# Latents' and grouped value projections placed behind the first scores of their attentions, keys ahead of queries

## The chip, the core and the metric

The program runs on one core of one Trainium2 chip. Five engines work side by side, each on its own stream of instructions, and meet only at semaphores: TensorE (PE) does matmuls and transposes, VectorE (DVE), ScalarE (ACT) and GpSimd (POOL) do the elementwise work, and SyncE (SP) issues the loads of the weights. The metric is the device time of one execution in microseconds (us); lower is better. Three runs of the kernel before gave 2188.7, 2191.41 and 2195.02, so the median is 2191.41.

## What is computed

The program runs two blocks one after the other. The first (window attention, memory attention, routed experts, twice) is not touched. The second works on 256 latent tokens and 256 context tokens of 1024 values in two layers. The part that matters here:

```python
h  = modulate(rmsnorm(x,  norm1_g[i]), sh1,  sc1)      # latents
hc = modulate(rmsnorm(xc, norm1_g[i]), csh1, csc1)     # context
# layer 0: differential attention, 8 heads, each with two maps of 64 values
q, k, v = split(t @ w_in, 3)           # for t = h and for t = hc
q, k = axial_rope(rmsnorm(q, q_norm)), axial_rope(rmsnorm(k, k_norm))   # latents only
a = softmax(q0 k0') - lam * softmax(q1 k1')
o = rmsnorm(a @ v, subln) * (1 - lambda_init)          # y = o @ w_out
# latents attend to context and latents (512 keys), the context to itself (256)
# layer 1: grouped attention, 8 query heads of 128 values over 2 key heads; only the latents' output
s = softmax(q k' / sqrt(128)); o = s @ v
```

Behind each attention comes `w_out`, a gated residual, a norm and a gated feed-forward network.

## The kernel before

All products of activations and weights are float32 in three passes: the weights and the activations are split in a high part (`w_hi`, `at_hi`) and a rest (`w_lo`, `at_lo`). A weight tile is 128x2048 floats (1 MB). SP loads it in one of 4 `raw` slots, ACT makes `w_hi` (L1426), POOL makes `w_lo` (L644, four pieces), and PE uses it from a ring of 3 slots. A tile is one quarter of a 1024x1024 projection.

The order of the work is written out by hand, once per engine, and every engine runs its stream in that order. In layer 0 (`context_and_latents`) it is:

1. the context's values (`gemm`), its keys (`heads_t(4, 0, ...)`), the transposes of the latents' normed rows into `at_hi`/`at_lo` (`to_at(HL)`), one small transpose (`columns`, L959), and the context's queries (`heads_t(0, 4, ...)`);
2. the context's attention (`diff_attention(0)`), after which DVE norms its output rows (L2177 to L2185, 128x1024 each, once per row tile) and transposes feed them to a second pair of activations;
3. the latents' values V1 (`gemm(1)`), the transposes of the context's output (`to_at(HC)`), the latents' values V2, the context's output projection D1, `tables(0)`, the second half D2, then the latents' four key tiles K0 to K3 and four query tiles Q0 to Q3 in one call, `heads_t(4, 4, 0, True)`;
4. the transposes of the context rows for its feed-forward, and the latents' attention (`diff_attention(1)`).

`heads_t` runs a tile's matmuls (`gemm_t`), ACT writes squares and a copy of them (L1697, L1699), and one tile later PE sums the squares with `ones` (L784 for a key, L791 for a query) and, with `turned`, multiplies by `swap` (L794) for the rope: `sums(j)`. For a key ACT takes the root (L1687), and DVE then works L2199, L2206 twice, L2210 and L2211; for a query DVE works L2206 twice and L2213, and one column scale at the end (L2224, L2225) serves all queries.

The bank ring: the results of `gemm_t`, of transposes and of scores go to four PSUM banks in turn. `wb_wait` lets PE write the n-th only when DVE (or the softmax) has freed the one four before it; `wb_freed` counts the freed ones in order. So a transpose behind three key tiles needs the first of them to be through DVE, and so on.

`tables(0)` spreads the rope table: DVE copies `TAB` into `PB` twice (L2235), PE transposes four pieces (L810), and DVE copies the result back (L2238). PE stands at `transpose_src()` until DVE has signalled.

`attention` is a pipeline over 16 pairs of head and row tile: in step `it` PE does the scores of `it` (L979; L1385 in layer 1), the transposes of the probabilities of `it-2` (L902) and the product with the values of `it-3` (L988, L1396). DVE takes maxima (L2302, L2326), ACT exponentials (L1564), DVE combines (L2343, L2354). Layer 1 runs `to_at(HL)`, one value tile (`gemm(1, 256)`), `tables(1)`, one key tile and four query tiles (`heads_t(1, 4, 1, True)`) and then its attention.

Of the kernel before, what the change touches and what calls it, by code (L numbers as in the profile page):

```python
# [31 lines left out]
P = 128  # L32
TOK = 256
NT = TOK // P
D = 1024
# [35 lines left out]
def gated_tiles(n_f):  # L71
# [8 lines left out]
         + 6 + 4 + gated_tiles(F_FFN // P))  # L80

# [99 lines left out]
def build(nc, A, out):  # L181
    ctx = ExitStack()
    with ctx:
# [136 lines left out]
        def q_bank(k_tiles):  # L320

            return head_bank(k_tiles, 0)
# [103 lines left out]
        def _(sp):  # L426
# [186 lines left out]
            by256(diff_in, 0, D)  # L613
            gemm(diff_in, 2 * D, 3 * D)
            gemm(diff_out, 0, D)
            by256(diff_in, D, 2 * D)
            by256(diff_in, 0, D)
# [4 lines left out]
            cols256(gqa_in, D + 256)  # L622
            cols256(gqa_in, D)
            by256(gqa_in, 0, D)
            gemm(gqa_out, 0, D)
# [40 lines left out]
        def _(pe):  # L666
# [104 lines left out]
            def heads_t(k_tiles, q_tiles, wide, turned, at=0, odd=0):  # L771


                freed, free = c.get("wb"), c.get("y")

                def sums(j):
# [4 lines left out]
                    if j >= 2:  # L781
                        pe.wait_ge(wb_freed, freed + j - 1)
                    if j < k_tiles:
                        ins = pe.matmul(head_bank(j + odd, 0), ones[wide][:, :], head_squares[j % 2], start=True, stop=True)  # L784
                    else:
                        per = 1 if wide else 2
                        own = ones[wide][:, 0:1] if wide else ones[wide][:, 0:P:64]
                        for b in range(2):
                            for t in range(NT):
                                c0 = t * 16 + (2 * (j - k_tiles) + b) * per  # L790
                                ins = pe.matmul(q_bank(k_tiles)[:, c0:c0 + per], head_squares[j % 2][:, b * TOK + t * P:b * TOK + (t + 1) * P],  # L791
                                                own, start=True, stop=True)
                    if turned:
                        ins = pe.matmul(head_bank(j, 1), swap[wide][:, :], head_rows[j % 2], start=True, stop=True)  # L794
# [9 lines left out]
            def tables(wide):  # L804
# [3 lines left out]
                for j in range(4):  # L808
                    src = TAB[:, j % 2 * 256 + j // 2 * P:j % 2 * 256 + j // 2 * P + P] if wide else PB[:, 0, j * P:(j + 1) * P]
# [77 lines left out]
            def attention(n, s_groups, scores, n_chunks, pv, fill=None, queries_last=False):  # L887
# [85 lines left out]
            def diff_attention(path):  # L973
# [18 lines left out]
                attention(16, 2, scores, lambda i: nk // P, pv, queries_last=True)  # L992

            def context_and_latents():
# [5 lines left out]
                columns(1)  # L1000
                heads_t(0, 4, 0, False, at=1)
                diff_attention(0)

                pe.wait_ge(y_freed, c.get("y"))
# [374 lines left out]
            gemm(1, 256)  # L1379
            tables(1)  # L1380
            heads_t(1, 4, 1, True)
# [19 lines left out]
            attention(16, 1, scores, lambda i: 4, pv, queries_last=True)  # L1401
# [7 lines left out]
        def _(act):  # L1409
# [267 lines left out]
            def heads_t(k_tiles, q_tiles, wide, turned, odd=0):  # L1677
# [29 lines left out]
                if q_tiles:  # L1707
                    act.wait_ge(head_summed, c.get("head"))
                    n = q_tiles * (4, 2)[wide]
                    nc.scalar.activation(q_scale[:, :, 0:n], q_bank(k_tiles)[:, 0:NT * 16].rearrange("p (t h) -> p t h", t=NT)[:, :, 0:n],  # L1710
                                         ACT.Sqrt, scale=1.0 / (64, P)[wide], bias=ms[:, 4:5]).then_inc(head_root, 1)

            def diff_attention(path):
                nk = TOK * (1 + path)
                attention(16, 2, lambda i: nk, "diff", None, chunks=lambda i: nk // P)
# [5 lines left out]
            def context_and_latents():  # L1721
# [9 lines left out]
                plain(1)  # L1731
                c.add("wb")
                heads_t(0, 4, 0, False)
                diff_attention(0)
                c.add("y", 2)
                tiles(2)
                to_at(at=1)
                act.dma_start(XC, A["ctx_2"][0].rearrange("(t p) d -> p t d", p=P)).then_inc(x_landed, 16)
                tiles(2)
                c.add("y", 2)  # L1740
                tiles(2)
                plain(1)
                c.add("wb")
                tiles(2)
                rms(XC)
                prm()
                heads_t(4, 4, 0, True)
# [136 lines left out]
            c.add("y", 1)  # L1884
            prm()
            tiles(1)
            plain(1)
            heads_t(1, 4, 1, True)
# [997 lines left out]
```

## Time and profile before

| what | value |
|---|---|
| median of three runs | 2191.41 us (2188.7 to 2195.02) |
| the profiled execution, first to last instruction | 2187.5 us |
| PE busy / DVE / ACT / POOL, us of the span | 1962.1 / 746.8 / 737.2 / 1008.6 |
| mean granted clock of TensorE | 0.944 of full speed |
| layer 0's attention of the context on PE | 1190 to 1231 |
| from there to the latents' attention | 1232 to 1346 |
| latents' attention | 1346 to 1406 |
| layer 1, from its transposes to the end of its attention | 1840 to 1951 |

The profile gives no time of its own for the profiled execution beside the span; the span is 3.9 us under the median of the runs. The stretches that the change touches lie between 1148 and 1406 and between 1840 and 1951. Times in the text are us from the start of the span. A row of a timeline reads: start, duration, engine, line, operation, result, inputs, shapes and count, and in brackets the idle time before it with the engine and line that ended it. A clock of 1.00 is 2.4 GHz, 0.50 is 1.2 GHz, and a value between them is a stretch that saw both.

### The profile page before, as it was taken

What the parts mean: (1) busy time and instruction counts of PE and PEld (TensorE: products, weight loads), DVE (VectorE), ACT (ScalarE), POOL (GpSimd) and SP (SyncE); (2) the same over time, 40 slices, a digit from 0 to 9 for tenths busy, and PEclk for the clock granted to TensorE, in tenths of its full rate; (3) what the DMA queues carried; (4) which work ended last, traced back from release to release, by engine and by line L of the source; (5) the groups of instructions that cost most, each with busy time, mean ns of one, the idle gap of its engine ahead of it and who ended that gap; (6) DMA issues with size and microseconds to landing.
All of it is one profiled execution on the core that took longest, in us unless ns stands there. A gap on an engine that the chain in (4) does not pass through costs nothing. (4 is left out here: it accounts for less than half of the span.)

```text
span 2187.5 us, 29236 instructions
## 1 busy us (share of the span) xinstructions
PE 1962.1 (90%) x11525; PEld 1488.9 (68%) x11525; DVE 746.8 (34%) x1336; ACT 737.2 (34%) x1026; POOL 1008.6 (46%) x784
## 2 busy tenths in 40 slices
PE   7879888999789997999887898999999997887998
PEld 5556654555367774554476686789988997767997
DVE  3453232111433133111244777821163214533112
ACT  3332320011233231111134545544364444444342
POOL 6326500000345630000174284088888886516886
PEclk9979998999899998999997998999999999998999
DMA  7535668999857649999953153056565665304662
GB/s 260 191 115 199 235 253 340 409 409 409 301 205 251 237 169 382 409 409 409 367 167 116 58 184 96 1 155 190 181 181 174 181 190 169 116 10 135 183 185 95
DMA packets 294981, 477.02 MB, mean 218 GB/s; under 512 B 16762, under 2 KB 196973, under 8 KB 294733
## 3 DMA queue, kind: packets, MB, share of 16 engines
q1 hardware_dynamic: 288812, 459.82, 59.5%
q10 hardware_dynamic: 6048, 15.53, 2.0%
q8 instruction: 84, 1.38, 0.3%
q14 instruction: 37, 0.30, 0.0%
HBM read 474.15 MB, written 1.15 MB: 217 GB/s over the span
## 5 line engine op out<-in xcount | busy, mean ns | idle before, releaser
L644 POOL TENSOR_TENSOR w_lo<-raw,w_hi 128x512 fp32r<-128x512 f32 x780 | 1008.4, 1327 | 1162.4 <-ACT w_hi L1426 1162.4
L710 PE MATMUL PS<-at_hi,w_hi 128*128 128x256 f32 x1680 | 488.4, 291 | 20.8 <-DVE at_lo L1935 16.9
L1426 ACT ACTIVATE w_hi<-raw 128x2048 fp32r<-128x2048 f32 x195 | 371.7, 1908 | 344.2 <-PE PS L712 335.8
L711 PE MATMUL PS<-at_lo,w_hi 128*128 128x256 f32 x1680 | 481.2, 286 | 0.0
L712 PE MATMUL PS<-at_hi,w_lo 128*128 128x256 f32 x1680 | 481.1, 286 | 0.0
L710 PEld LDWEIGHTS PS<-at_hi,w_hi 128*128 128x128 f32 x1680 | 328.7, 196 | 35.4 <-DVE at_lo L1935 16.3
L711 PEld LDWEIGHTS PS<-at_lo,w_hi 128*128 128x128 f32 x1680 | 328.7, 196 | 3.7 <-issue 2.6
L712 PEld LDWEIGHTS PS<-at_hi,w_lo 128*128 128x128 f32 x1680 | 328.3, 195 | 0.0
L710 PE MATMUL PS<-w_hi,at_hi 128*128 128x512 f32 (+1 forms) x480 | 192.6, 401 | 31.3 <-DVE at_lo L1935 13.7
L711 PE MATMUL PS<-w_lo,at_hi 128*128 128x512 f32 (+1 forms) x480 | 187.8, 391 | 0.0
L712 PE MATMUL PS<-w_hi,at_lo 128*128 128x512 f32 (+1 forms) x480 | 187.6, 391 | 0.0
L2259 DVE TENSOR_TENSOR PB<-PB,PS 128x256 f32<-128x256 f32 x66 | 27.8, 421 | 363.6 <-ACT PB L1513 363.4
L710 PEld LDWEIGHTS PS<-w_hi,at_hi 128*128 128x128 f32 x480 | 94.8, 198 | 67.7 <-issue 18.3
L712 PEld LDWEIGHTS PS<-w_hi,at_lo 128*128 128x128 f32 x480 | 94.4, 197 | 18.5
L711 PEld LDWEIGHTS PS<-w_lo,at_hi 128*128 128x128 f32 x480 | 95.1, 198 | 17.4 <-issue 0.2
L710 PE MATMUL PS<-w_hi,he_hi 128*128 128x512 f32 x264 | 103.2, 391 | 0.0
L711 PE MATMUL PS<-w_lo,he_hi 128*128 128x512 f32 x264 | 103.1, 390 | 0.0
L712 PE MATMUL PS<-w_hi,he_lo 128*128 128x512 f32 x264 | 102.7, 389 | 0.0
L1145 PE MATMUL PS<-w_plain_hi,KT 128*64 128x512 f32 x224 | 99.2, 593 | 2.0 <-issue 1.2
L678 PE MATMUL PS<-raw,spread_c 128*8 128x512 f32 x384 | 77.2, 700 | 26.1 <-DMA raw<-ada_w 24.6
L1145 PE MATMUL PS<-w_plain_lo,KT 128*64 128x512 f32 x224 | 99.5, 594 | 0.0
L2622 DVE SCALAR_TENSOR_TENSOR at_hi<-PS,st,at_hi 128x1024 fp32r<-128x1024 f32 x16 | 20.5, 1284 | 217.7 <-ACT at_hi L1602 217.7
(312 smaller groups left out, 2499.9 us busy)
## 6 DMA issues: line engine op xcount, KB each, us to landing
raw<-ffn_w_gu SPq DMA_DIRECT2D x132, 512.0 KB, 5.0
raw<-ada_w SPq DMA_DIRECT2D x64, 768.0 KB, 5.3
raw<-ffn_w_down SPq DMA_DIRECT2D x66, 512.0 KB, 4.1
raw<-l_e_up SPq DMA_DIRECT2D x48, 512.0 KB, 15.1
raw<-diff_w_in SPq DMA_DIRECT2D x48, 512.0 KB, 4.6
raw<-l_xkv SPq DMA_DIRECT2D x32, 512.0 KB, 5.6
w_plain_hi<-l_e_gate SPq DMA_DIRECT2D x32, 512.0 KB, 15.0
w_plain_lo<-l_e_gate SPq DMA_DIRECT2D x32, 512.0 KB, 15.3
```

The costliest lines, as they stand in the source:

```text
L644: ins = nc.gpsimd.tensor_tensor(w_lo[:, n % RING, part], raw[:, order_of(n) % RAW, part], w_hi[:, n % RING, part].bitcast(F32), ALU.subtract)
L678: ins = pe.matmul(mod_bank[32 * n:32 * n + 8, :], spread_c[:, a % MOD_TILES, :], raw[:, s % RAW, n * 512:(n + 1) * 512], start=a % MOD_TIL ...
L710: pe.matmul(dst, s_hi, m_hi, start=first, stop=False)
L711: pe.matmul(dst, s_hi, m_lo, start=False, stop=False)
L712: return pe.matmul(dst, s_lo, m_hi, start=False, stop=last)
L1145: ins = pe.matmul(PS[r, bank, :], xe[p % 2][:, 4 * h + k, r], tiles[e][:, k * 512:(k + 1) * 512], start=h == 0 and k == 0, stop=h == 1 and ...
L1426: nc.scalar.activation(w_hi[:, n % RING, :], raw[:, s % RAW, :], ACT.Copy).then_inc(hi_done, 1)
L2259: freed(dve.tensor_tensor(h, silu_buf[:, f % 2, :], b[:, TOK:2 * TOK], ALU.mult))
L2622: dve.scalar_tensor_tensor(o_parts[1].rearrange("p (m n) -> p m n", m=2), PS[:, 6:8, :], st[:, p % 2, 0:1], o_parts[0].bitcast(F32).rearra ...
```

## The change

It moves work and adds a few waits; no product is added or dropped.

- `tables(0)` goes from between D1 and D2 to ahead of the context's queries.
- After the context's attention come K0, K1 and K2, then the transposes of the context's output, then K3, D1, D2 and Q0 to Q3. Before it was V1, transposes, V2, D1, D2, K0 to K3, Q0 to Q3.
- V1 is issued behind the first scores of the latents' attention (`it == 0`) and V2 behind the second (`it == 1`); DVE copies each out to `V` at the same step.
- Layer 1's value tile goes behind the first scores of its attention.
- The `swap` products of the queries all go to one bank, beside the one with the queries' sums, so that `sums(j)` of a query now waits until DVE has freed the tile before it (`freed + j` where it was `freed + j - 1` from `j >= 2`).
- SP loads the weight tiles in the new order.

```diff
-            by256(diff_in, D, 2 * D)
-            by256(diff_in, 0, D)
-            gemm(diff_in, 2 * D, 3 * D)
-            gemm(diff_out, 0, D)
             by256(diff_in, D, 2 * D)
+            gemm(diff_out, 0, D)
             by256(diff_in, 0, D)
+            gemm(diff_in, 2 * D, 3 * D)
...
-                    if j >= 2:
+                    if j >= 1 and j >= k_tiles:
+                        pe.wait_ge(wb_freed, freed + j)
+                    elif j >= 2:
                         pe.wait_ge(wb_freed, freed + j - 1)
...
+                    if it < len(values):
+                        if it:
+                            pe.wait_ge(wb_freed, queries_done)
+                            pe.wait_ge(head_root, c.get("root"))
+                        values[it]()
                     if queries_last and it == 2:
                         pe.wait_ge(wb_freed, queries_done)
+                    if values and it == 2:
+                        pe.wait_ge(y_freed, c.get("y"))
...
                 columns(1)
+                tables(0)
                 heads_t(0, 4, 0, False, at=1)
                 diff_attention(0)
...
-                gemm(1)
-                to_at(HC, wait=False)
-                gemm(1)
-                at_wait()
-                gemm(1, at=1)
-                tables(0)
-                gemm(1, at=1)
-                heads_t(4, 4, 0, True)
+                heads_t(3, 0, 0, True)
+                to_at(HC, wait=False)
+                heads_t(1, 0, 0, True, odd=1 - Y_OUT)
+                pe.wait_ge(wb_freed, c.get("wb") - 1)
+                gemm(1, at=1)
+                at_wait()
+                pe.wait_ge(head_root, c.get("root"))
+                gemm(1, at=1)
+                heads_t(0, 4, 0, True, q_pair=1 - Y_OUT)
                 to_at(HL, wait=False)
                 diff_attention(1)
...
             to_at(HL)
-            gemm(1, 256)
             tables(1)
-            heads_t(1, 4, 1, True)
+            heads_t(1, 4, 1, True, q_pair=1 - Y_GROUPED)
```

Line numbers of the changed kernel differ: its L737 is L730 here, its L820 is L810, L794 is L784, L804 is L794, L996 is L979, and its L717 to L719 are L710 to L712.

On PE, ahead of the context's queries (the transposes of `H` end `to_at(HL)`; `mod_in` and `QT` belong to `columns`). Before:

```order
L730 MATMUL PS<-ident,H 128x128 [waits wb_freed]
L730 MATMUL PS<-ident,H 128x128 x3
L959 MATMUL PS<-ident,QT 128x96 [waits wb_freed,mod_in]
L710 MATMUL PS<-at_hi,w_hi 128x256 [waits lo_done,wb_freed]
L711 MATMUL PS<-at_lo,w_hi 128x256
```

and in the changed kernel:

```order
L737 MATMUL PS<-ident,H 128x128 [waits wb_freed]
L737 MATMUL PS<-ident,H 128x128 x3
L976 MATMUL PS<-ident,QT 128x96 [waits wb_freed,mod_in]
L820 MATMUL PS<-ident,PB 128x128 [waits wb_freed,src_ready]
L820 MATMUL PS<-ident,PB 128x128 x3
L717 MATMUL PS<-at_hi,w_hi 128x256 [waits lo_done,wb_freed]
L718 MATMUL PS<-at_lo,w_hi 128x256
```

The four transposes of the table, with their wait for DVE's two copies, now stand in front of the first query tile.

On DVE, behind the norm of the context's output (its last two operations are the first two rows). Before, the values, the transposed output and the table come next, and the keys much later:

```order
L2182 TENSOR_TENSOR H<-H,hs 128x1024
L2185 TENSOR_TENSOR H<-H,bc 128x1024
L2158 COPY V<-PS 128x512 x2
L1935 TENSOR_TENSOR at_lo<-PS,at_hi 128x4x128 x4
L2158 COPY V<-PS 128x512 x2
L2235 COPY PB<-TAB 128x256 x2
L2238 COPY TAB<-PS 128x512
L2111 TENSOR_TENSOR PB<-PS,PRM 128x512 x2
```

and in the changed kernel, from the third key on (K0 and K1 stand before it in the same four kinds of rows):

```order
L2225 RECIPROCAL PT<-PT 128x512
L2232 SCALAR_TENSOR_TENSOR PT<-PS,gains,TAB 128x512 x2
L2236 TENSOR_TENSOR PT<-PT 128x512
L2237 TENSOR_TENSOR KT<-PT 128x2x256
L1961 TENSOR_TENSOR at_lo<-PS,at_hi 128x4x128 x4
L2225 RECIPROCAL PT<-PT 128x512
```

Three keys' work now lies between the norm and the four `at_lo` of the context's output, and the fourth key's behind them.

On PE, at the head of the latents' attention. Before (the last transposes of the context's rows, then scores of three steps):

```order
L730 MATMUL PS<-ident,H 128x128 x3
L979 MATMUL PS<-KT,QT 128x512 [waits wb_freed,y_freed]
L979 MATMUL PS<-KT,QT 128x512 [waits wb_freed] x5
L902 MATMUL PS<-ident,PB 128x128 [waits t_freed,p_ready,wb_freed]
L902 MATMUL PS<-ident,PB 128x128 x3
```

and in the changed kernel:

```order
L737 MATMUL PS<-ident,H 128x128 x3
L996 MATMUL PS<-KT,QT 128x512 [waits wb_freed,y_freed]
L996 MATMUL PS<-KT,QT 128x512 [waits wb_freed]
L717 MATMUL PS<-w_hi,at_hi 128x512 [waits lo_done,y_freed]
L718 MATMUL PS<-w_lo,at_hi 128x512
```

After the first step's two maps V1 begins (96 matmuls); V2 stands likewise behind the second step's.

## Rows read from the trace of the kernel before

**Rows 1.** The page: the span.

```profile
span 2187.5 us, 29236 instructions
```

**Rows 2.** Busy time by stretch; columns as in the first line.

```profile
core 0: us, PE busy (x) PEld busy (x) DVE busy (x) ACT busy (x) POOL busy (x), PEclk, DMA share, GB/s
1232.00:1278.30 46.30, 46.10 (x214) 38.41 (x215) 26.75 (x27) 15.69 (x13) 34.80 (x27) 1.00 0.48 155
...
1346.50:1363.60 17.10, 14.83 (x32) 6.29 (x32) 12.20 (x27) 12.03 (x27) 0.00 (x0) 0.50 0.14 39
...
1850.30:1860.00 9.70, 8.40 (x49) 8.21 (x49) 0.92 (x4) 1.18 (x1) 0.00 (x0) 0.72 0.20 75
```

**Rows 3.** Timeline of PE ahead of the context's queries.

```profile
1152.57 1.09 PE L730 MATMUL PS<-ident,H 128*128 128x128 f32 x4 [3.28 <-DVE KT L2215]
...
1162.30 0.58 PE L710 MATMUL PS<-at_hi,w_hi 128*128 128x256 f32 x1 [2.38 <-DVE at_lo L1935]
```

**Rows 4.** Timeline of DVE there: the copy of `columns`.

```profile
1164.39 0.26 DVE L2413 COPY modcol<-PS 128x96 f32<-128x96 f32 x1
```

**Rows 5.** The line of the table's copies: ns min/median/max, first and last start.

```profile
L2235 DVE COPY PB<-TAB x2: 1261/3718/6175, 1257.6 to 1263.8; 128x256 f32<-128x256 f32 x2
```

**Rows 6.** Timeline of POOL, near 1164 and during those copies.

```profile
1172.61 2.55 POOL L644 TENSOR_TENSOR w_lo<-raw,w_hi 128x512 fp32r<-128x512 f32 x2 [17.61 <-ACT w_hi L1426]
...
1254.84 13.92 POOL L644 TENSOR_TENSOR w_lo<-raw,w_hi 128x512 fp32r<-128x512 f32 x11
```

**Rows 7.** Timeline of PE behind the context's attention: V1.

```profile
1232.20 0.47 PE L710 MATMUL PS<-w_hi,at_hi 128*128 128x512 f32 x1 [1.04 <-issue]
...
1243.21 1.91 PE L730 MATMUL PS<-ident,H 128*128 128x128 f32 x16
```

**Rows 8.** Timelines of ACT and DVE there: the norm's ends.

```profile
1240.71 0.21 ACT L1471 ACTIVATE hs<-hs 128x8 f32<-128x8 f32 x1 [5.58 <-DVE hs L2179]
...
1242.52 1.22 DVE L2185 TENSOR_TENSOR H<-H,bc 128x1024 f32<-128x1024 f32 x1
```

**Rows 9.** Timeline of PE in the latents' keys.

```profile
1278.13 0.28 PE L710 MATMUL PS<-at_hi,w_hi 128*128 128x256 f32 x1
...
1290.96 0.68 PE L710 MATMUL PS<-at_hi,w_hi 128*128 128x256 f32 x1
...
1298.42 0.68 PE L710 MATMUL PS<-at_hi,w_hi 128*128 128x256 f32 x1
```

**Rows 10.** Timeline of ACT in the keys: the copies, then a split.

```profile
1289.84 0.60 ACT L1697 ACTIVATE PB<-PS 128x512 f32<-128x512 f32 x1 [1.34 <-PE PS L712]
...
1292.15 1.90 ACT L1426 ACTIVATE w_hi<-raw 128x2048 fp32r<-128x2048 f32 x1
```

**Rows 11.** Timeline of DVE: the norm behind D2, then keys.

```profile
1287.61 0.75 DVE L2143 TENSOR_SCALAR H<-H,mv 128x1024 f32<-128x1024 f32 x1
...
1300.17 3.35 DVE L2199 RECIPROCAL PT<-PT 128x512 f32<-128x512 f32 x1
...
1307.65 3.35 DVE L2199 RECIPROCAL PT<-PT 128x512 f32<-128x512 f32 x1
```

**Rows 12.** Timeline of DVE: the last query and the queries' scale.

```profile
1339.52 1.54 DVE L2206 SCALAR_TENSOR_TENSOR PT<-PS,gains,TAB 128x512 f32<-128x512 f32 x2
...
1342.69 0.87 DVE L2225 TENSOR_SCALAR q_scale<-q_scale 128x32 f32<-128x32 f32 x1
```

**Rows 13.** Timeline of PE: the start of the latents' attention.

```profile
1346.49 6.89 PE L979 MATMUL PS<-KT,QT 64*128 64x512 f32 x8 [3.39 <-DVE at_lo L1935]
...
1363.62 0.97 PE L979 MATMUL PS<-KT,QT 64*128 64x512 f32 x2
```

**Rows 14.** Timeline of PE in layer 1.

```profile
1850.36 0.58 PE L710 MATMUL PS<-w_hi,at_hi 128*128 128x256 f32 x1 [8.62 <-DVE at_lo L1935]
...
1859.95 0.66 PE L810 MATMUL PS<-ident,TAB 128*128 128x128 f32 x4 [1.23 <-DVE hs L2231]
...
1906.15 1.09 PE L902 MATMUL PS<-ident,PB 128*128 128x128 f32 x4 [5.47 <-DVE st L2351]
```

**Rows 15.** Timeline of DVE in layer 1: the key begins.

```profile
1874.67 3.35 DVE L2199 RECIPROCAL PT<-PT 128x512 f32<-128x512 f32 x1 [13.26 <-ACT PT L1687]
```

More of the change, by code:

```diff
@@ L769, in gemm_t, with heads_t @@
                     tile_end(ins)
-            def heads_t(k_tiles, q_tiles, wide, turned, at=0, odd=0):
+            def heads_t(k_tiles, q_tiles, wide, turned, at=0, odd=0, q_pair=0):
                 freed, free = c.get("wb"), c.get("y")
+                c.add("root", k_tiles + (q_tiles > 0))
                 def sums(j):
@@ L885, in gated, with attention @@
                 dn(False, True)
-            def attention(n, s_groups, scores, n_chunks, pv, fill=None, queries_last=False):
+            def attention(n, s_groups, scores, n_chunks, pv, fill=None, queries_last=False, values=()):
                 pe.wait_ge(y_freed, c.get("y"))
@@ L991, in pv @@
                         ins.then_inc(o_full, 1)
-                attention(16, 2, scores, lambda i: nk // P, pv, queries_last=True)
+                values = (lambda: gemm(1), lambda: gemm(1)) if path else ()
+                attention(16, 2, scores, lambda i: nk // P, pv, queries_last=True, values=values)
             def context_and_latents():
@@ L1378, in _ @@
             to_at(HL)
-            gemm(1, 256)
             tables(1)
-            heads_t(1, 4, 1, True)
+            assert c.get("y") % 2 == Y_GROUPED
+            heads_t(1, 4, 1, True, q_pair=1 - Y_GROUPED)
             def scores(i, _, bank):
@@ L1400, in pv @@
                     ins.then_inc(o_full, 1)
-            attention(16, 1, scores, lambda i: 4, pv, queries_last=True)
+            attention(16, 1, scores, lambda i: 4, pv, queries_last=True, values=(lambda: gemm(1, 256),))
             pe.wait_ge(y_freed, c.get("y"))
@@ L1714, in diff_attention, with values @@
                 nk = TOK * (1 + path)
-                attention(16, 2, lambda i: nk, "diff", None, chunks=lambda i: nk // P)
+                def values(it):
+                    if path and it < 2:
+                        c.add("y")
+                        tiles(2)
+                attention(16, 2, lambda i: nk, "diff", None, chunks=lambda i: nk // P, fill=values)
                 c.add("y", 4)
@@ L1883, in _, with values @@
             to_at(shifts(0, 1, 0))
-            c.add("y", 1)
             prm()
-            tiles(1)
             plain(1)
-            heads_t(1, 4, 1, True)
-            attention(16, 1, lambda i: 512, "gqa", None, o_at=lambda i: i % 4 == 3, chunks=lambda i: 4,
+            heads_t(1, 4, 1, True, q_pair=1 - Y_GROUPED)
+            def values(it):
+                if it == 0:
+                    c.add("y")
+                    tiles(1)
+            attention(16, 1, lambda i: 512, "gqa", None, o_at=lambda i: i % 4 == 3, chunks=lambda i: 4, fill=values,
                       evac=lambda i: (at_hi[:, 2 * (i // 4):2 * (i // 4) + 2, :], o_bank().rearrange("p (k q) -> p k q", k=2)))
@@ L2185, in head_norm, with heads_t @@
                     (ready if signal else D1)(dve.tensor_tensor(v[:, t, :, :], v[:, t, :, :], g, ALU.mult))
-            def heads_t(k_dsts, q_dsts, gain, wide, turned):
+            def heads_t(k_dsts, q_dsts, gain, wide, turned, odd=0, q_pair=0):
                 first, freed_before = c.get("head"), c.get("wb")
@@ L2287, in gated, with attention @@
                     dve.wait_ge(tile_used, c.get("tile"))
-            def attention(n, s_groups, nk, kind, scale, o_at, o_evac):
+            def attention(n, s_groups, nk, kind, scale, o_at, o_evac, values=()):
                 t0 = c.get("t")
@@ L2361, in attention @@
                         norm(it - 1)
+                    if it < len(values):
+                        values[it]()
                     if 0 <= it - 3 < n and o_at(it - 3):
@@ L2459, in o_evac @@
                                              head_weights[:, own].unsqueeze(2).to_broadcast([P, 4, P]), ALU.mult))
-                attention(16, 2, lambda i: nk, "diff", None, lambda i: i % 4 == 3, o_evac)
+                values = [lambda n=n: y_to([V[:, 2 + u, n * 512:(n + 1) * 512] for u in range(NT)]) for n in range(2 * path)]
+                attention(16, 2, lambda i: nk, "diff", None, lambda i: i % 4 == 3, o_evac, values)
                 dve.wait_ge(y_freed, c.get("y"))
@@ L2811, in _ @@
             dve.wait_ge(tab_landed, 16 * 8)
-            y_to([V[:, 2 + t, 0:256] for t in range(NT)], 256, 1)
-            settled()
             tables(1)
-            heads_t([KT[:, 0:2, TOK:2 * TOK]], [QT[:, 2 * j:2 * j + 2, :] for j in range(4)], G_GK, 1, True)
+            heads_t([KT[:, 0:2, TOK:2 * TOK]], [QT[:, 2 * j:2 * j + 2, :] for j in range(4)], G_GK, 1, True,
+                    q_pair=1 - Y_GROUPED)
             def o_evac(i):
@@ L2819, in o_evac @@
                 o_split(at_hi[:, 2 * j:2 * j + 2, :], at_lo[:, 2 * j:2 * j + 2, :], 2)
-            attention(16, 1, lambda i: 512, "gqa", None, lambda i: i % 4 == 3, o_evac)
+            attention(16, 1, lambda i: 512, "gqa", None, lambda i: i % 4 == 3, o_evac,
+                      [lambda: y_to([V[:, 2 + t, 0:256] for t in range(NT)], 256, 1)])
             a, b8 = affine_of(0, 1, 1)
```

58 lines of the change are left out of this document (29 added, 29 removed).

## The prediction

> **What bounds the kernel now.** I read the page first: the span is 2187.5 us [rows 1], 3.9 under the median of 2191.41, and the chain that ended last is nearly all TensorE. The sum below is a difference inside the profiled execution, added to that median. PE is busy in nearly all of the span, so the question is where it stands still, and at which clock it runs behind that. Second I read PE's waits by stretch, third the timelines of PE and DVE there. What the reader is to see: between the context's attention and the last query PE works without a pause, 46.10 of 46.30 us at clock 1.00 in its first half [rows 2]. It stands still in front of the latents' attention, whose start then runs at clock 0.50 from 1346.5 to 1363.6 with 14.83 of 17.10 us busy [rows 2, 13]. Layer 1 has the same: 8.62 us of waiting, a slow value tile, and 5.47 us of waiting behind the first scores [rows 14]. The change aims the value projections at these holes. They are 22 us and 5.8 us of matmuls, and they do not get shorter by moving; a gain is only what they cover. In their old places they covered something too: DVE's norm of the context's output, and its copies of the table. So I price three places.
>
> **Place 1, the table, ahead of the context's queries.** Before, the first query tile began at 1162.30, behind a wait for `at_lo` [rows 3]. Now PE must also wait for DVE: its copy for `columns` ends at 1164.39 + 0.26 = 1164.65 [rows 4], then come two copies of the table, then PE's transposes, whose start lies 0.42 ahead of the first product in layer 1 (1859.95 there [rows 14]). The delay is (1164.65 - 1162.30) + copies + 0.4 = 2.75 + copies. The copies are the unknown. Before they took 1.26 and 6.18 us for the same 128x256 elements [rows 5], with POOL at work without a gap from 1254.84 for 13.92 us; around 1164 POOL has been idle for most of the 17.61 us that end at 1172.61, as it waits for ACT, which waits for PE [rows 6]. Lower bound: the 0.26 of the 128x96 copy [rows 4] twice, rounded to 0.5. Upper bound: the 7.4 of before. I take 1.2, nearer to the quiet row, since the same copy cannot need both 1.26 and 6.18 for its own work. So +4.0, between +3.3 and +10.2. The old place cost PE nothing (it ran D1 above it), so nothing comes back.
>
> The Trainium skill bears on this ("SBUF — State Buffer", SBUF: two separate sides): VectorE and GpSimd share a port pair as an exclusive lock, and an fp32 copy within SBUF is of the kind that needs it. By that rule the 6.18 is waiting for POOL's pieces, the trace's spread agrees, and place 1 costs the lower figures; without it the delay would be near 10.
>
> **Place 2, keys ahead of values in the latents' part.** I follow both engines from 1231.2, where the attention's last product ends. PE: K0, K1 and the first sums take 12.8 (1278.13 to 1290.96), each further key 7.5 (1290.96 to 1298.42) [rows 9]: 1244.0, then 1251.5. DVE norms the context's output until 1243.7 and ACT is held by it until 1240.9 [rows 8]; ACT then needs two copies of 1.1, a split of 1.9 [rows 10] and a root of 0.7, 4.9 in all, so K0 begins on DVE at 1245.9. A turned key costs DVE 7.5 (1300.17 to 1307.65) [rows 11], as much as PE. So DVE stays late: K0 done at 1253.4, K1 at 1260.9, K2 at 1268.4. Before, PE's 22 us of values gave DVE the time to catch up.
>
> Who waits for it: the transposes of the context's output. The bank ring lets the second to the fourth group of four go only after K0, K1 and K2; that the ring does this is seen ahead of the context's queries, where such a group waited 3.28 for `KT` [rows 3]. PE, free at about 1255, is held until 1268.4. K3's tile wants the bank of the first group, which DVE empties 0.7 later: 1269.1. Behind so long a hole the clock has fallen: in layer 1 one tile behind 8.62 us of waiting took 8.4 at clock 0.72 [rows 2, 14] instead of 5.8. So K3 ends at 1277.5. Then ACT's copies, for which there is no second tile to cover, 1.3, and the sums, 1.3: D1 begins at 1280.1. D1 and D2 are 11.0 each, as V1 was (1232.20 to 1243.21) [rows 7]: 1302.1. DVE's gate and norm behind D2 took until 1288.36 after 1278.13 [rows 9, 11], 10.2, here 1312.3, under the first query tiles. Q0, Q1 and sums: 1314.9; Q2: 1322.4; Q3 with the sums of Q2 (1.8, estimated as a key's with eight small products): 1330.3. The new wait holds the last sums until DVE is through Q2, 2.9: 1333.2; they end at 1335.0, and the last query with the scale takes DVE 4.1 (1339.52 to 1343.56) [rows 12]: 1339.1, which is 4.5 ahead of before.
>
> Now the attention. The scores began 2.9 behind the scale (1346.49) [rows 12, 13]: 1342.0. Two maps at the low clock, the second waiting for its bank, 3.1; V1, 11.0 and 2.6 for the clock as above: 1358.7. Scores 1.2, V2 11.0: 1370.9. Then scores, DVE's copy of V2, one maximum, transposes and the first product with V: I take 6.3, between the 4.2 that this work is at full clock (half of the 8.4 it was busy at clock 0.50) and the 17.1 of the ramp before [rows 2]. The scores of the fifth step begin at 1377.2, before at 1363.62 [rows 13]: +13.6. POOL now works during the first steps and slows DVE's operations a little, +0.4: +14.0. In words: 22 us of values went into the ramp and filled only some 9 of it, and the hole that they left cost more. If the K0 to K2 chain is 3 us shorter or longer, so is this.
>
> **Place 3, layer 1.** The value tile's 9.6 us (1850.36 to 1859.95) [rows 14] leave the front, but its slow start passes to the key: -9.5 + 2.6 = -6.9. The key's sums then run 6.9 earlier, DVE's work on it too: 1874.67 - 6.9 + 7.8 = 1875.6 [rows 15]; the first query's sums, which had no such wait, are due at about 1872.6: +2.9. The last query waits like the latents': +2.9 on PE. Its scale ends at about 1901, 2.5 ahead. Then the value tile, 5.8, stands in the hole of 5.47 [rows 14]; DVE copies it before the second maximum, and the first transposes go at about 1905.7, before at 1906.15. With the better clock behind it: -1.0, between -4 and +3.
>
> **The sum.** 4.0 + 14.0 - 1.0 = +17.0, so 2191.41 + 17.0 = 2208.4; I say 2208. The weights hide: POOL had 17.61 us to spare at place 1, and a hole at PE only lets it get ahead.
>
> **Rivals.**
> A, not slower: the hole between K2 and K3 does not open. It decides at the fourth group of transposes: if DVE is through K2 by 1256 and not at 1268.4, K3 starts at once, its tile runs at full clock and D1 begins 16.6 earlier. Then place 2 is -2.6, the sum +0.4: 2192. For it: 30 us of DVE's work in these keys holds long reciprocals that some other work might let start earlier. Against it: the stream is in order, DVE's norm cannot move, and 7.5 per key stands in four rows running.
> B, slower still: the table's copies take 7.4 as before. It decides on whether the 6.18 was POOL or the operation: sum +23, 2214. Against it are the two durations of one operation.
> C, the low clock stays longer, as it did for the 17.1 us of the ramp, behind the hole in the keys or under V1. By the Trainium skill ("TensorE: Matmul & The Clock Gate", What's actually happening) activity releases the clock again, and a dense tile should recover; rows 2 agree for one tile (0.72). If not, K3, D1's start and V1 give some 4 more: 2212.
> D, the change gives more in the ramp than I credit: the 6.3 is 4.2, the holes are 3 us less. 2202.
>
> **Chances.** Forecast 2208 (2204 to 2211) 0.53; A 0.12; B 0.12; C 0.11; D 0.12. The range takes D, C and B in and leaves A out: 2199 to 2216. About 0.3% (6.6 us) is what a measurement of this kernel can tell from no change. A splits into 0.05 faster and 0.07 within it, and D leaves 0.02 within it: faster 0.05, same 0.09, slower 0.86.
>
> **What would show it.** Right: PE waits of 5 to 15 us at the transposes L737 released by `KT`, a low clock in the key tile behind them, the fifth step's scores 17 to 19 later than before, and L820's wait ending near 1166. Wrong: no wait there, two copies of the table above 5 us, or the first transposes of layer 1's attention earlier than 1903. If the sum is missed by more than 8 us, I expect the DVE chain of K0 to K2 to be the step that failed.

## The result and the profile after

The changed kernel took 2209.86 us (median of 4 runs, 2208.03 to 2210.82); the kernel before took 2190.05 (4 runs, 2185.65 to 2195.02). The ratio is 1.0091 with a 95% interval of 1.0074 to 1.0108: slower, by 16 to 24 us. The forecast was 2208, +17. The page of the kernel after begins:

```profile
span 2208.9 us, 29236 instructions
```

The profiled execution spans 21.4 us more than the one of before [rows 1], with as many instructions and the same mean clock of 0.944. I place the time by the same event in both traces. Up to the transposes for `columns`, which end the stretch that is alike in both, the kernel after is already 1.66 us late (1161.19 against 1159.53). The five other runs of this study that have no change of their own ahead of it stand there between 4.81 early and 2.05 late, so this is scatter of single executions and I subtract it. The rest:

| place | ends with | lateness there, less what came before it |
|---|---|---|
| 1, the table | the last product of the context's attention | 5.87 - 1.66 = +4.2 |
| 2, the latents' part | the first transposes of layer 1 | 18.42 - 5.87 = +12.6 |
| 3, layer 1 | the first tile behind its attention | 21.35 - 18.42 = +2.9 |

**Place 1.** DVE ahead of the context's queries, a timeline of the kernel after (start, duration, engine, line and operation, and in brackets the idle time before it with what ended it):

```profile
1165.27 0.69 DVE L1961 TENSOR_TENSOR at_lo<-PB,at_hi 128x512 fp32r<-128x512 f32 x1 [1.36 <-ACT at_hi L1493]
1166.05 0.26 DVE L2441 COPY modcol<-PS 128x96 f32<-128x96 f32 x1
1166.34 0.62 DVE L2261 COPY PB<-TAB 128x256 f32<-128x256 f32 x2
```

and PE there, and at the last query's sums:

```profile
1167.02 1.11 PE L820 MATMUL PS<-ident,PB 128*128 128x128 f32 x4 [5.43 <-DVE PB L2261]
1167.79 0.56 PE L717 MATMUL PS<-at_hi,w_hi 128*128 128x256 f32 x1
...
1195.92 1.02 PE L801 MATMUL PS<-ones,PB 128*128 128x2 f32 x8 [1.01 <-DVE QT L2243]
```

The two copies, which took 1.26 and 6.18 us before [rows 5], take 0.62 together. POOL has nothing to do beside them:

```profile
1151.72 4.93 POOL L651 TENSOR_TENSOR w_lo<-raw,w_hi 128x512 fp32r<-128x512 f32 x4 [1.60 <-ACT w_hi L1445]
1177.65 5.04 POOL L651 TENSOR_TENSOR w_lo<-raw,w_hi 128x512 fp32r<-128x512 f32 x4 [20.99 <-ACT w_hi L1445]
```

The first query tile begins at 1167.79, 5.49 later than in [rows 3], or 3.8 less the 1.66. The 1.01 at the last query is the new wait on the tile before it; the prediction had no term for it here. The first query tiles run 0.45 shorter and the attention wins back a little, and so the place costs 4.2.

**Place 2.** The keys on DVE, each one a reciprocal, two products with the table, a sum and a product:

```profile
1252.00 3.35 DVE L2225 RECIPROCAL PT<-PT 128x512 f32<-128x512 f32 x1 [2.39 <-ACT PT L1706]
...
1257.75 1.64 DVE L2237 TENSOR_TENSOR KT<-PT 128x512 f32<-128x512 f32 x1
1259.47 3.35 DVE L2225 RECIPROCAL PT<-PT 128x512 f32<-128x512 f32 x1
...
1267.21 3.35 DVE L2225 RECIPROCAL PT<-PT 128x512 f32<-128x512 f32 x1
...
1272.89 0.69 DVE L2237 TENSOR_TENSOR KT<-PT 128x512 f32<-128x512 f32 x1
1273.62 2.87 DVE L1961 TENSOR_TENSOR at_lo<-PS,at_hi 128x512 fp32r<-128x512 f32 x4
```

PE beside it (`L737` are the transposes of the context's output, `L717` at 1274.40 begins K3):

```profile
1259.54 1.10 PE L794 MATMUL PS<-PB,ones 128*128 128x512 f32 x2 [0.89 <-DVE KT L2237]
...
1267.32 1.09 PE L737 MATMUL PS<-ident,H 128*128 128x128 f32 x4 [4.95 <-DVE KT L2237]
1273.64 1.12 PE L737 MATMUL PS<-ident,H 128*128 128x128 f32 x4 [5.23 <-DVE KT L2237]
1274.40 0.56 PE L717 MATMUL PS<-at_hi,w_hi 128*128 128x256 f32 x1
```

DVE goes from one key to the next without a pause, and PE stands still three times, 11.1 us in all, each time until a key is done. In the old order PE was busy for 46.10 of 46.30 us here [rows 2]. The windows of the kernel after that answer to [rows 2] (start:end, length, busy us of PE, of its loads, of DVE, ACT and POOL with counts, clock, DMA share, GB/s):

```profile
1261.30:1274.40 13.10, 2.92 (x17) 2.27 (x16) 12.72 (x12) 2.26 (x4) 5.33 (x4) 0.69 0.50 160
1347.30:1364.20 16.90, 16.09 (x54) 11.06 (x54) 4.73 (x9) 8.68 (x15) 3.34 (x3) 0.80 0.01 1
1364.20:1384.00 19.80, 16.61 (x78) 11.60 (x77) 12.46 (x20) 10.29 (x14) 17.53 (x14) 1.00 0.52 159
```

In the first of them PE is busy for 2.92 of 13.10 us while DVE is busy for 12.72: that is how a reader sees who is bound by whom. The other two are the ramp of the latents' attention with V1 and V2 in it. It runs at a clock of 0.80 and 1.00 instead of 0.50, but it is 36.7 us long instead of 17.1:

```profile
1347.34 1.20 PE L996 MATMUL PS<-KT,QT 64*128 64x512 f32 x2 [2.33 <-DVE at_lo L1961]
...
1364.14 1.13 PE L996 MATMUL PS<-KT,QT 64*128 64x512 f32 x4
...
1376.32 1.13 PE L996 MATMUL PS<-KT,QT 64*128 64x512 f32 x4
...
1384.00 1.17 PE L996 MATMUL PS<-KT,QT 64*128 64x512 f32 x4 [0.89 <-DVE head_sums L2365]
```

The fifth step's scores begin at 1384.00 where they began at 1363.62 [rows 13], +14.5 less the 5.87 of before. The rest of the attention takes 41.5 us instead of 42.5, with the clock at 1.00 instead of 0.95, and the stretch behind it 0.9 less (44.5 at 0.96 against 45.4 at 0.92). That leaves the 12.6. These two gains are no scatter: the rest of the attention takes 41.1 to 41.5 us in the three traces that have V1 and V2 in the ramp and 42.5 to 42.7 in the seven others, and the stretch behind it is 0.9 shorter in the same three alone.

**Place 3.** PE in layer 1, from the first query's sums on (`L801` and `L804` belong to `sums`, `L1404` are scores, `L912` the first transposes of the probabilities):

```profile
1893.80 1.35 PE L801 MATMUL PS<-ones,PB 128*128 128x1 f32 x8 [3.01 <-DVE KT L2237]
1895.01 2.05 PE L804 MATMUL PS<-PB,swap 128*128 128x512 f32 x2
1896.07 1.20 PE L717 MATMUL PS<-at_hi,w_hi 128*128 128x256 f32 x1
...
1917.12 1.02 PE L801 MATMUL PS<-ones,PB 128*128 128x1 f32 x8 [3.20 <-DVE QT L2239]
...
1919.64 1.91 PE L1404 MATMUL PS<-KT,QT 128*128 128x512 f32 x2
1920.57 1.20 PE L717 MATMUL PS<-w_hi,at_hi 128*128 128x256 f32 x1
...
1930.09 0.63 PE L912 MATMUL PS<-ident,PB 128*128 128x128 f32 x4 [0.97 <-DVE PB L2380]
```

The hole of 5.47 us in [rows 14] is 0.97 now, filled by the value tile. In its stead stand two new waits of 3.01 and 3.20 us. The windows behind each, and of the attention's rest, show what else they cost:

```profile
1896.00:1905.90 9.90, 9.90 (x61) 9.14 (x59) 2.19 (x3) 1.20 (x3) 2.73 (x3) 0.74 0.45 163
1917.10:1927.30 10.20, 10.18 (x61) 8.14 (x62) 3.44 (x7) 2.43 (x4) 3.44 (x3) 0.83 0.46 127
...
1930.00:1974.10 44.10, 35.79 (x154) 22.98 (x155) 23.86 (x63) 22.70 (x50) 5.03 (x4) 1.00 0.08 25
```

The attention's rest in the kernel before, to be held against the last row:

```profile
1906.10:1952.80 46.70, 39.23 (x155) 25.55 (x155) 23.36 (x63) 22.59 (x49) 0.00 (x0) 0.92 0.06 16
```

PE is busy throughout the first two and yet slow, at clocks of 0.74 and 0.83. A query tile takes 8.4 us (1896.07 to 1904.50), and the next one 6.1 (1905.86 to 1912.00).

### The profile page after: what moved, and what is told of

It reads as the page before. It is cut to its first block and busy times, and to the rows that moved or that the text cites. A ratio compares the mean times of both kernels' runs of the same rounds, so it can differ in the third digit from the quotient of the medians.

```text
span 2208.9 us, 29236 instructions
## 1 busy us (share of the span) xinstructions
PE 1961.2 (89%) x11525; PEld 1486.6 (67%) x11525; DVE 737.9 (33%) x1336; ACT 737.7 (33%) x1026; POOL 1007.5 (46%) x784
## 5 line engine op out<-in xcount | busy, mean ns | idle before, releaser
L717 PE MATMUL PS<-at_hi,w_hi 128*128 128x256 f32 x1680 | 490.1, 292 | 18.4 <-DVE at_lo L1961 14.5
L719 PE MATMUL PS<-at_hi,w_lo 128*128 128x256 f32 x1680 | 482.8, 287 | 0.0
L717 PEld LDWEIGHTS PS<-at_hi,w_hi 128*128 128x128 f32 x1680 | 330.9, 197 | 32.3 <-DVE at_lo L1961 13.7
L719 PEld LDWEIGHTS PS<-at_hi,w_lo 128*128 128x128 f32 x1680 | 330.2, 197 | 0.0
L717 PE MATMUL PS<-w_hi,at_hi 128*128 128x512 f32 (+1 forms) x480 | 194.4, 405 | 21.9 <-POOL w_lo L651 9.3
L719 PE MATMUL PS<-w_hi,at_lo 128*128 128x512 f32 (+1 forms) x480 | 187.6, 391 | 0.0
L717 PEld LDWEIGHTS PS<-w_hi,at_hi 128*128 128x128 f32 x480 | 94.6, 197 | 60.6 <-issue 25.0
L719 PEld LDWEIGHTS PS<-w_hi,at_lo 128*128 128x128 f32 x480 | 94.2, 196 | 18.9
L717 PE MATMUL PS<-w_hi,he_hi 128*128 128x512 f32 x264 | 103.2, 391 | 0.0
L719 PE MATMUL PS<-w_hi,he_lo 128*128 128x512 f32 x264 | 102.7, 389 | 0.0
```

What stands on the lines that cost most here:

```text
L717: pe.matmul(dst, s_hi, m_hi, start=first, stop=False)
L719: return pe.matmul(dst, s_lo, m_hi, start=False, stop=last)
```

## The experiments

Ratios are to the kernel before on the same chip, with 95% intervals. On the first chip (table alone, no reciprocal, layer 1 alone, layer 1 free of both waits) it took 2188.57 (24 runs), on the second (the other four) 2187.95 (29 runs). The changed kernel was not run on these two, so where a run is held against it, two ratios are compared. A time behind a ratio is the ratio less 1, times the time of the kernel before. Next to each stands the effect read from the trace, freed of the scatter ahead of the touched place as above.

**The table alone.** The kernel before with only place 1 of the change.

```diff
                 columns(1)
+                tables(0)
                 heads_t(0, 4, 0, False, at=1)
...
                 gemm(1, at=1)
-                tables(0)
                 gemm(1, at=1)
```

> The kernel before with one part of the change alone: the rope table's work (two copies and one on DVE, four transposes on PE) ahead of the context's queries. Theory (place 1): the copies are short there since POOL is idle, as the trace of the changed kernel shows (0.62 us for both), so PE's first query tile starts 3.8 us later and nothing comes back at the old place: about +4 us against before. Rival 1: the old place gives something back, as DVE was blocked for 7.5 us there and so late for the keys: +0 to +2. Rival 2: place 1 is larger than it looks in a trace with both parts: +6 or more.

Measured: 2191.41, ratio 1.0015 (1.0002 to 1.0028), +3.3 us; by the trace +3.2 at the end. PE ahead of the queries:

```profile
1163.97 1.12 PE L810 MATMUL PS<-ident,PB 128*128 128x128 f32 x4 [5.43 <-DVE PB L2234]
1164.74 0.56 PE L710 MATMUL PS<-at_hi,w_hi 128*128 128x256 f32 x1
```

The wait is the same 5.43, and the first query tile is 3.8 late as in the changed kernel. It lacks the queries' new wait, so it does not rise to 4.2 but falls to 3.5 by the context's scores. The timed interval, +0.4 to +6.1, would leave room for both rivals; it is the trace that shows the term.

**The table hidden.** The copies stand on DVE between the context's two value copies, the transposes on PE ahead of the context's keys.

```diff
                 gemm(2, at=1)
+                tables(0, ahead=NT)
                 heads_t(4, 0, 0, False, at=1)
...
                 gemm(1, at=1)
-                tables(0)
                 gemm(1, at=1)
```

> The kernel before, with the copies of the context queries' table put on VectorE between the first two copies of the context's values, and TensorE's transposes of its columns ahead of the context's keys, where both engines have other work in hand. Everything else is as before. Theory (place 1 of the change costs 3 to 4 us only because the two copies and the transposes between them stand in line just ahead of the queries' first tile): hidden like this the time is within 0 to +0.7 us of the kernel before. Rival (the cost is in the queries' new order, or the table is needed earlier than it comes): +3 us, as with the table's part of the change alone.

Measured: 2188.44, ratio 1.0006 (0.9991 to 1.0021), +1.3 us (-2.0 to +4.6), which alone does not exclude the rival's +3. By the trace it is +0.2 behind the transposes for `columns`, and the first query tile begins 2.77 us behind them, as in the kernel before. That count leaves out the table's new place, which lies ahead of them; counted from an event ahead of that (1086.41 against 1083.97) it is +0.9, with PE's waits for POOL's `w_lo` in between, which differ from trace to trace. The two copies took 1.27 us each there and PE did not wait for them. So most of the cost of place 1 is its position, directly ahead of a tile that waits for DVE anyway.

**No reciprocal for the latents' first three keys.** The changed kernel with DVE's chain K0 to K2 shortened by some 10 us; the three keys are scaled by the root itself, so the output differs.

```diff
-                        D1(dve.reciprocal(head_rstd[j % 2], head_rstd[j % 2]))
+                        if len(k_dsts) != 3:
+                            D1(dve.reciprocal(head_rstd[j % 2], head_rstd[j % 2]))
```

> The changed kernel without the reciprocal of the norms of the latents' first three key tiles (3.35 us each on DVE), so that keys are scaled by the root instead of by its inverse. Theory (place 2 is the chain of DVE's work on K0 to K2): DVE is through K2 some 9 to 10 us earlier, the waits of the last transposes before K3 shrink by as much, and K3's tile runs at a better clock: 10 to 12 us faster than the changed kernel, so about 8 us above the kernel before. Rival (the hole comes from DVE's norm of the context's output and ScalarE's start behind it, which stay): 3 us or less faster than the changed kernel.

Measured: 2203.97 (6 runs), ratio 1.0078 (1.0062 to 1.0094), where the changed kernel has 1.0091: some 3 us faster, with intervals that overlap. By the trace, place 2 is +6.0 instead of +12.6, 6.5 less; but the profiled execution is the fastest of the six (2199.82), so the size lies between 3 and 7. The three waits become two, 2.57 and 3.85 us or 6.4 in all instead of 11.1:

```profile
1258.24 0.63 PE L737 MATMUL PS<-ident,H 128*128 128x128 f32 x4 [2.57 <-DVE KT L2238]
1262.71 1.11 PE L737 MATMUL PS<-ident,H 128*128 128x128 f32 x4 [3.85 <-DVE KT L2238]
```

The 10 to 12 us of my theory missed either way. DVE's timeline says why:

```profile
1253.91 1.54 DVE L2233 SCALAR_TENSOR_TENSOR PT<-PS,gains,TAB 128x512 f32<-128x512 f32 x2 [2.87 <-ACT PT L1706]
...
1256.45 1.64 DVE L2238 TENSOR_TENSOR KT<-PT 128x512 f32<-128x512 f32 x1
1258.12 1.54 DVE L2233 SCALAR_TENSOR_TENSOR PT<-PS,gains,TAB 128x512 f32<-128x512 f32 x2
```

Without the reciprocals DVE waits 2.87 us for K1, whose sums PE makes only 7.5 us behind K0's. Once the chain on DVE is short, PE's own pace of a tile and its sums is the limit: K2 is done 30.3 us behind the context's attention instead of 36.5, which is 6.3 of the 10 us taken out. So the reciprocals are a part of the hole, as the shorter waits show. That the 6.4 us that stay come from the order itself, which puts the transposes right behind the sums of the keys that free their banks, is read from the timelines and was not tried alone; the next run changes that order.

**Values split.** The kernel before with the table hidden, and in the latents' part V1, the transposes, K0, D1, D2, K1 to K3, Q0 to Q3, scores, scores, V2.

```diff
                 gemm(1)
                 to_at(HC, wait=False)
-                gemm(1)
-                at_wait()
+                heads_t(1, 0, 0, True)
+                pe.wait_ge(wb_freed, c.get("wb") - 1)
                 gemm(1, at=1)
+                at_wait()
+                pe.wait_ge(head_root, c.get("root"))
                 gemm(1, at=1)
-                heads_t(4, 4, 0, True)
+                heads_t(3, 4, 0, True)
...
+                          values=(lambda: None, late_values) if path else ())
```

> The kernel before with the table hidden as in the run above, and in the last block's latents an order in between: first head's values, the transposes to the context's part, the first key and the shared tiles between (D1, D2), then the other three keys together, all four queries, the transposes to the latents, scores; only the second values' matrix goes behind the second scores. Keys come ahead of queries as in the change, but the keys' normalisation has other tiles' work beside it. Theory (place 2 costs 12.6 us because three keys' normalisations in a row leave TensorE waiting 11 us, and because 10 us of values' products that covered them went behind the scores): with the products D1, D2 and V1 beside the keys, the time is 2 to 4 us below the kernel before. Rival (putting values behind the scores costs by itself, since the attention waits for them or for the banks): 2 to 6 us above it.

Measured: 2191.01, ratio 1.0019 (1.0004 to 1.0034), +4.1 us; by the trace +3.0 in the latents' part, and +2.5 from the transposes for `columns` to the end of all that it touches (which leaves out the hidden table, as above). My expectation was wrong in sign. PE, at the new place of K0 and at the scores:

```profile
1243.52 0.39 PE L712 MATMUL PS<-at_hi,w_hi 128*128 128x256 f32 x1 [1.63 <-DVE at_lo L1955]
...
1250.87 1.10 PE L787 MATMUL PS<-PB,ones 128*128 128x512 f32 x2 [1.33 <-ACT PB L1716]
...
1335.35 6.89 PE L987 MATMUL PS<-KT,QT 64*128 64x512 f32 x8 [3.39 <-DVE at_lo L1955]
1342.17 0.79 PE L712 MATMUL PS<-w_hi,at_hi 128*128 128x512 f32 x1
```

and the window of V2 behind the scores:

```profile
1342.10:1355.60 13.50, 13.50 (x51) 10.65 (x50) 2.53 (x6) 4.68 (x9) 3.37 (x3) 0.82 0.00 0
```

The long waits of the keys are gone, and with them three quarters of what place 2 cost. Two short ones of 1.63 and 1.33 us are left, where V2 stood before. But V2 takes 13.4 us at clock 0.82, and not the 11.0 of its old place, while the ramp without it shrinks only from 15.3 to 12.9 us (first scores to first product with V, less V2). So the ramp hides 2.4 us of it and the low clock takes 2.4 back, and the two short waits, 3.0 us together, are what the part costs. That is the second finding on place 2: even without the long hole in the keys, this value projection gains nothing in the ramp.

**Layer 1 alone.** The kernel before with only place 3 of the change. The diff is that of the change for layer 1, with `if wide and j >= 1 and j >= k_tiles` for the new wait.

> The kernel before with layer 1's part alone: the value tile behind the first scores, and one bank for all the queries' swap products, with its stricter waits. My theory now, from the trace of the changed kernel: PE waits 3.0 us for the key's work and 3.2 for the last query but one, and the tile behind the first of these waits runs at the low clock; +3 us against before. Rival (as predicted): the waits cost their own length only and the value tile fills the hole in the softmax's start, -1 us.

Measured: 2192.7, ratio 1.0023 (1.0014 to 1.0032), +5.0 us (3.1 to 7.0); by the trace +2.8, as in the changed kernel (+2.9). Slower, not 1 us faster: the prediction's term has the wrong sign. The waits of 3.0 and 3.2 us stand at the same two places. The first of them and what follows it:

```profile
1870.17 1.18 PE L797 MATMUL PS<-ones,PB 128*128 128x1 f32 x8 [3.01 <-DVE KT L2224]
...
1872.28 1.20 PE L714 MATMUL PS<-at_hi,w_hi 128*128 128x256 f32 x1
```

The wait is the same, but the sums and the tile behind it take 10.5 us (to 1880.71), where they took 12.1 in the changed kernel (1893.80 to 1905.86) and take 8.9 when nothing waits. So the slow work behind a wait of 3.01 us cost 3.2 us in one trace and 1.7 in the other.

**No wait for the key's work.** The changed kernel, but layer 1's key is put in the other pair of banks, so that the first query's sums need not wait for it.

```diff
-                    if j >= 1 and j >= k_tiles:
+                    if j > k_tiles:
                         pe.wait_ge(wb_freed, freed + j)
...
-            heads_t(1, 4, 1, True, q_pair=1 - Y_GROUPED)
+            heads_t(1, 4, 1, True, odd=1, q_pair=1 - Y_GROUPED)
```

> The changed kernel, with one thing undone in layer 1 of the last block: its key's work goes through the other pair of banks, and waits for it only before the latents' tiles, so that the grouped query's products no longer wait 3.0 us behind the first four key tiles. Theory (the changed kernel's place 3 came out at +2.9 us and not -1.0, because each of the two waits of some 3 us is followed by tiles at the low clock, 8.4 us for one that takes 6.2 elsewhere): without the wait, its 3.0 us and about as much of low clock go, 5.5 to 6 us faster than the changed kernel, so about 2204. Rival (only the length of the wait counts, the low clock there has another cause): 3 us faster. Second rival (the wait only moves to the next place, the query's work): 0 to 1 us faster.

Measured: 2201.52 (6 runs), ratio 1.0058 (1.0041 to 1.0075) against 1.0091, or 7 us faster with intervals that just touch. By the trace, from the transposes of layer 1 to the tile behind its attention: 109.4 us instead of 116.0, so -6.7. The theory had -5.5 to -6, the length of the wait alone -3. The window that answers to 1896.00:1905.90 above:

```profile
1891.30:1899.00 7.70, 7.70 (x63) 7.22 (x61) 6.11 (x6) 2.89 (x3) 7.02 (x6) 1.00 0.41 136
```

The clock there is 1.00, and the tile with its sums takes 7.5 us (1892.67 to 1900.17), where it took 9.8 (1896.07 to 1905.86). The wait for the last query (3.20) stays. That the low clock goes with the wait is shown by the two traces. The size is less firm: 6.7 is the difference of two executions, the timed difference lies between some 2 and 12 us, and the run with layer 1 alone has 3.0 + 1.7 for the same wait.

**Layer 1 free of both waits.** The kernel before with layer 1's value tile behind the scores as in the change, the queries' sums in the bank of the key's sums as soon as ACT has taken the key's root, and the `swap` products in turn in two banks again, so that none waits for the tile just before it. One of the two belongs to the value tile later, which therefore waits for the last query but one.

```diff
+            return PS[:, 0, :] if wide else head_bank(k_tiles, 0)
...
+            return head_bank(j + odd, 1)
...
+                        if wide and j == k_tiles:
+                            pe.wait_ge(head_root, first_root)
...
                     if it < len(values):
+                        pe.wait_ge(wb_freed, queries_done - 1)
                         values[it]()
```

> As the run with layer 1's part alone, but the two waits are taken away by their cause: key and queries go on alternating between the two swap banks, the queries' sums share the key's bank once ScalarE has taken the root, and the value tile waits for the last query but one, which comes late enough anyhow. Theory (the loss is the waits and the clock behind them): no PE wait above 1 us between the first key product and the first scores, the clock stays 1.00 there, and the kernel is 5 to 6 us faster than before. Rival (moving a value tile behind the scores is no gain in itself, as its 5.8 us come back where they go): within 2 us of before.

Measured: 2178.51 (7 runs), ratio 0.9964 (0.9949 to 0.998), -7.9 us; by the trace -7.7. This kernel beats both. The windows with the value tile (first row), and from the first query's tile to the scores:

```profile
1886.00:1898.00 12.00, 10.53 (x66) 7.94 (x66) 10.54 (x17) 6.09 (x8) 6.88 (x5) 1.00 0.62 174
1862.70:1888.00 25.30, 25.30 (x188) 22.72 (x186) 15.68 (x14) 11.54 (x14) 18.58 (x14) 1.00 0.41 142
```

PE does not stop once in 25.3 us, and the value tile runs at full clock. The idea of place 3 is good; the banks that it was given undid it. Theory -5 to -6: right in sign, somewhat small.

**Both.** Values split and layer 1 free in one kernel, the edits of the two sections above.

> The run above together with layer 1's keys and queries freed of their waits (keys first, each kind of work in banks of its own), which alone gave -7.9 us. Theory (the two places are apart in time and add up): 10 to 12 us below the kernel before, so about 2178 at its 2188.6. Rival (the gain of the latents' order is taken back by a lower clock in layer 1): no more than 8 us below.

Measured: 2185.32, ratio 0.9989 (0.9977 to 1.0001), -2.4 us. The expectation rested on a gain of the split values that is not there. The two places do add up: 1.0019 and 0.9964 make 0.9983, within the interval, and by the trace it is -5.0 for +2.5 and -7.7; so the second half of the theory held, and the latents' order is better left as it was.

## Why the prediction held

Each step of place 2, with the changed kernel's times less 5.87 beside the forecast:

| step | forecast | trace |
|---|---|---|
| K0 begins on DVE | 1245.9 | 1246.1 |
| DVE is through K2 | 1268.4 | 1267.7 |
| K3's tile begins | 1269.1 | 1268.5 |
| D1 begins | 1280.1 | 1278.2 |
| the latents' scores begin | 1342.0 | 1341.5 |
| V1 ends | 1358.7 | 1358.3 |
| V2 ends | 1370.9 | 1370.5 |
| fifth step's scores | 1377.2 | 1378.1 |

**Place 2 is right in mechanism and size:** +14.5 at the fifth step against +13.6. D1 came 1.9 us earlier, because the key tile behind the hole took 6.9 us and not 8.4, and the ramp behind V2 took 7.7 and not 6.3. What I left out is the clock behind: 1.0 and 0.9 us came back, so +12.6 and not +14.0.

That the scores begin within 0.5 us of the forecast is in part luck, as two errors cancel there. The last sums, behind the new wait of 3.20, took 3.5 us (1337.88 to 1341.35) and not 1.8, low clock that I had not charged. DVE's last query with the scale took 2.7 (1341.67 to 1344.41) and not 4.1.

**Place 1 is right:** +4.2 against +4.0, by quiet copies (0.62 for my 1.2), 0.77 for the table's transposes (my 0.4), and a wait at the last query (1.01) that I priced only in the other two places. Rival B, slow copies, fell with the 0.62. By the Trainium skill ("SBUF — State Buffer", SBUF: two separate sides) a copy of this kind waits only while GpSimd holds the port pair that they share; the trace agrees, with 0.62 us beside an idle POOL where [rows 5] have 1.26 and 6.18 beside a busy one. Why one of those took 6.18 no run shows: beside a busy POOL in the run with the table hidden both took 1.27.

**Place 3 is where the sum was mis-sized:** -1.0 forecast, +2.9 measured, inside my -4 to +3 at its very end. The step that failed is "the first transposes go at about 1905.7": they went at 1930.09 - 18.42 = 1911.7, 6.0 later. The waits were as forecast (3.01 and 3.20 for 2.9 each), and the key began 7.2 us earlier on DVE for my 6.9. Missing was the slow work behind each wait, though I had charged exactly this for the longer holes. Behind the first it is 2.3 us in the tile (8.43 for 6.14) and 0.9 in the sums ahead of it (1893.80 to 1896.07, against 1.36 for those that begin at 1904.50); with that the queries' scale ends at 1904.2 by the old count and not at 1901. Behind the second it is 0.8 in the last sums (1917.12 to 1919.64, where the kernel before needs 1.75), 0.1 in the scores and 0.8 in the value tile (6.7 for my 5.8), 1.7 together. The two make 4.9 of the 6.0. The rest lies in waits that were 0.4 longer and in the steps from the value tile to the transposes, 2.85 us that I priced too low. Of the 6.0, 2.0 came back, since the attention's rest ran at 1.00 and not at 0.92 and took 44.0 for 46.6 us, where I had counted 0.6. Removing one wait gave 6.7 us, removing both turned the place into a gain of 7.7.

**The sum:** 4.2 + 12.6 + 2.9 = 19.7, beside 19.8 between the medians. The parts of the sum missed by +0.2, -1.4 and +3.9, and in the total errors of opposite sign cancel in part. Rival A asked for K2 to be done by 1256; it was done at 1267.7 by the same count, and even without the reciprocals it is not before 1261.4. Rival C, a low clock that lasts under K3 and V1, is out, as both were on time; its mechanism showed in layer 1 instead. Rival D, more from the ramp, is out: the ramp took more.

## What to carry to other kernels

Before work is moved into a hole, ask what it covered where it stood: here 22 us of values hid two engines' normalisation, and the hole that they left cost more than the one that they filled gave. Where the clock falls behind a wait, charge more than its length (here 4.7 to 6.7 us for 3.0); so a bank shared by two tiles can cost more than the tile that was moved can gain. And when such a move fails, look for the resource that adds the wait before giving up the order: with the `swap` products in two banks instead of one, layer 1's part alone went from +2.8 to -7.7 us.

## What the runs showed of the hardware beside this

- DVE's product into `KT` took 1.64, 1.63 and 0.69 us for the same 128x512 elements. POOL worked from 1249.65 to 1266.63 without a long pause, and the third stands where it was idle again. The copies of the table behave alike: 0.62 us for two with POOL idle, 1.27 each and up to 6.18 with it at work. That two operands in SBUF alone set this is not shown here. The reciprocal took 3.35 us in each of the three, with POOL at work and idle.
- TensorE's clock fell behind a wait of 3.0 us (0.74 in the 9.9 us that follow it), and behind waits of 4.95 and 5.23 the next tile, 6.9 us long, was less slow than the 8.4 behind the shorter one. The length of the wait alone does not set it: in the run with layer 1 alone the wait was 3.01 again, with the same work ahead of it in layer 1, and the tile took 7.1. No run here takes this apart.
- A stretch of the same instructions took 45.4 or 44.5 us as the clock in it was 0.92 or 0.96, with no change to it: what was done ahead of a stretch moves its clock. It repeats: layer 1's attention, from its first transposes on, takes 44.0 us in the six traces that have the value tile behind the first scores and 46.6 in the four that do not.
